# Block 2's scan: C multiplied by decays spread over the partitions, in place of products that are scaled and turned

## The reference

```python
a_cs = jnp.cumsum(aq, axis=2)
seg = a_cs[:, :, :, None] - a_cs[:, :, None]
decay = jnp.exp(jnp.where(lower, seg, -jnp.inf))
scores = jnp.einsum('bcqgn,bcsgn->bcqsg', Cq, Bq)
y_diag = jnp.einsum('bcqsg,bcqsgr,bcsgrp->bcqgrp', scores, decay, xq)
y_off = jnp.einsum('bcqgn,bcgrpn,bcqgr->bcqgrp', Cq, h_in, jnp.exp(a_cs))
...
y = y + xs.reshape(b, L, SSD_HEADS, SSD_HEAD_DIM) * d_skip[:, None]
y = rms_norm_2(y * jax.nn.silu(z), g_ssd)
return jnp.concatenate([fourier_mix(u_f), y], axis=-1) @ w_out
```

## Time and profile before

| | |
|---|---|
| Time, median of 3 runs | 1623.92 us (1622.88 to 1626.29) |
| Profiled execution: own time, span | 1624.92 us, 1622.4 us |
| PE busy, weight loads | 1607.2 us (99%), 1541.8 us |
| DVE, ACT, POOL busy | 1293.1, 923.2, 210.2 us |
| Granted clock of PE | 0.999 |
| The scan on PE | 1372.54 to 1393.25 us of the span |

### The profile page before, as it was taken

The page is one execution under the profiler, slowest core; times in us unless marked ns, Lnnn a source line. Parts: engine busy times, 40 slices in busy tenths (PEclk is TensorE's granted clock), DMA queues, the critical chain, the costliest instruction groups (busy, mean ns, idle before and its releaser), DMA issues.

```text
span 1622.4 us, 29880 instructions
## 1 busy us (share of the span) xinstructions
PE 1607.2 (99%) x13136; PEld 1541.8 (95%) x13136; DVE 1293.1 (80%) x1463; ACT 923.2 (57%) x1096; POOL 210.2 (13%) x122
## 2 busy tenths in 40 slices
PE   8999999999999999999999999999999999999998
PEld 8999988999999999999987899999999989899998
DVE  8887878687889888897878688885999597796655
ACT  7554655684465455545556686464655567554544
POOL 1000100000040001200000000032323368400000
PEclk9999999999999999999999999999999999999999
DMA  8667654444566765776754444555555434235552
GB/s 296 229 259 279 246 181 168 146 155 158 214 229 235 269 250 199 267 260 254 282 184 165 147 157 156 185 219 191 190 201 182 145 118 155 79 131 190 200 186 75
DMA packets 47520, 317.56 MB, mean 196 GB/s; under 512 B 5280, under 2 KB 8096, under 8 KB 9888
## 3 DMA queue, kind: packets, MB, share of 16 engines
q1 hardware_dynamic: 47248, 315.64, 53.3%
q10 hardware_dynamic: 144, 0.02, 0.0%
HBM read 314.60 MB, written 1.05 MB: 195 GB/s over the span
## 4 chain that ended last, share of the span: by engine, by line
PE 82%; DVE 9%; ACT 4%; POOL 2%; DMA 1%; issue 1%; SPq 0%; DVEq 0%; ACTq 0%
PE ps L1170 23%; PE ps L1172 23%; PE ps L1171 23%; PE ps L1368 3%; PE ps L1370 3%; PE ps L1369 3%; DVE wlo L1844 2%; ACT whi L648 1%; DVE pre L2455 1%; DMA raw<-in_w_dram 1%; PE ps L1382 1%; DVE dA_rows L1844 1%; DVE tmp L1844 1%; PE ps L1393 1%; DVE qkA L1844 1%
## 5 line engine op out<-in xcount | busy, mean ns | idle before, releaser
L1844 DVE TENSOR_TENSOR wlo<-raw,whi 128x2048 fp32r<-128x2048 f32 (+1 forms) x256 | 585.0, 2293 | 92.8 <-ACT whi L648 89.3
L648 ACT ACTIVATE whi<-raw 128x2048 fp32r<-128x2048 f32 (+1 forms) x264 | 499.9, 1905 | 216.9 <-DMA raw<-in_w_dram 216.9
L1170 PE MATMUL ps<-h1hi,whi 128*128 128x256 f32 x1792 | 500.8, 279 | 2.9 <-DVE wlo L1844 2.9
L1172 PE MATMUL ps<-h1lo,whi 128*128 128x256 f32 x1792 | 496.7, 277 | 0.0
L1171 PE MATMUL ps<-h1hi,wlo 128*128 128x256 f32 x1792 | 496.6, 277 | 0.0
L1170 PEld LDWEIGHTS ps<-h1hi,whi 128*128 128x128 f32 x1792 | 337.0, 188 | 7.1 <-issue 4.2
L1172 PEld LDWEIGHTS ps<-h1lo,whi 128*128 128x128 f32 x1792 | 337.1, 188 | 0.0
L1171 PEld LDWEIGHTS ps<-h1hi,wlo 128*128 128x128 f32 x1792 | 336.8, 188 | 0.1
L1170 PE MATMUL ps<-hid_hi,whi 128*128 128x256 f32 x880 | 244.0, 277 | 0.0
L1172 PE MATMUL ps<-hid_lo,whi 128*128 128x256 f32 x880 | 243.4, 277 | 0.0
L1171 PE MATMUL ps<-hid_hi,wlo 128*128 128x256 f32 x880 | 243.4, 277 | 0.0
(11 more groups left out here) (363 smaller groups left out, 2536.5 us busy)
## 6 DMA issues: line engine op xcount, KB each, us to landing
raw<-in_w_dram SPq DMA_DIRECT2D x288, 1024.0 KB, 4.8
raw<-in_w_dram SPq DMA_DIRECT2D x8, 256.0 KB, 5.4
c_rows<-in_c_rows_dram SPq DMA_DIRECT2D x2, 1024.0 KB, 9.9
relbias<-in_relbias_dram SPq DMA_DIRECT2D x2, 1024.0 KB, 8.5
pv<-in_pv_dram SPq DMA_DIRECT2D x2, 641.0 KB, 7.5
xT<-in_x_dram SPq DMA_DIRECT2D x4, 256.0 KB, 4.6
raw<-in_w_dram SPq DMA_DIRECT2D x2, 512.0 KB, 7.1
ctxT<-in_ctx_dram SPq DMA_DIRECT2D x1, 1024.0 KB, 6.9
```

The costliest lines, as they stand in the source:

```text
L648: act.activation(whi[:, slot, c], raw[:, slot, c], ACT.Copy).then_inc(hi_done[slot], 1)
L1170: pe.matmul(out, w_hi, hi, start=start, stop=False, skip_group_check=skip)
L1172: return pe.matmul(out, w_hi, lo, start=False, stop=stop, skip_group_check=skip)
L1844: return dve.tensor_tensor(out, a, b, op)
```

## The change

- The running decays are no longer taken as 48 columns (`tail_x[:, 48:96]`), but as rows: after chunk 11's segments PE makes 12 x 512 sums in bank 7, ACT takes their exponentials (`decay_rows`), SP writes them to a DRAM tensor and reads them back spread over all 128 partitions, in four transfers of 3, 3, 2 and 1 heads and a fifth of 3 heads behind a wait for the last segment sums (`seg_done` 6). A head's 4 x 128 decays are 256 KB over the partitions, so three heads are 768 KB.
- The decays take one place of the weight ring: a pseudo slab (`FILL`) stands in the stream behind b2+10 and its slot is given back by carried(3). Slab b2+11 and all later ones move one slot on, and b2+11 is loaded behind the five transfers.
- DVE multiplies C by the decays (`c_decay(g)`, heads 3g to 3g+2, both operands in SBUF, in place): g = 0 after conv(11), g = 1 after conv(12) and `z_clamp(0)`, g = 2 behind `cut_lo(b2 + 11)`, g = 3 behind `h1_ready`.
- `carried(e)` becomes 12 products by head that accumulate in y's banks. `carried_scale`, `turned` and `yoff` are gone. PE's order is cb, carried(0) to carried(3), within(0), within(1), then within(2) and within(3) in turns of four heads.
- The skip term's product moves from DVE to ACT (six ACTIVATEs on `xs_t`); DVE's add becomes one instruction for two tiles.
- Orders: ACT's `cut_hi` of b2+11, W0, W1, W2 comes one odd chunk later each and W3's behind `z_sigmoid(2)`; POOL does z's first gate ahead of `xdt`; DVE does `z_clamp(1)` ahead of W0's `cut_lo`, all four `within_weights` (with `z_clamp(2)` behind the third) ahead of W1's.

```diff
+DECAYS = (None, 0)
-    after = {}
+    after = {BLOCK2_0 + 10: DECAYS}
@@ SP
+                if i == FILL:
+                    sp.wait_ge(decay_rows_ready, 1)
+                    sp.dma_start(decay_dram, decay_rows[0:NH, :, :].rearrange("h e n -> h (e n)")).then_inc(decays_moved, 16)
                 if n > 0:
                     sp.wait_ge(used[slot], n)
+                if i == FILL:
+                    sp.wait_ge(decays_moved, 16)
+                    spread(0, 3, landed[slot])
+                    spread(3, 6, block2_landed)
+                    spread(9, 11, block2_landed)
+                    spread(11, 12, block2_landed)
+                    sp.wait_ge(seg_done, 6)
+                    spread(6, 9, decays_moved)
@@ POOL
+        z_gate(0)
         for tt in range(ST):
             ...
-        for j in range(3):
-            ...
+        z_gate(1)
+        cut_lo(b2 + WOUT20 + 2)
+        z_gate(2)
         cut_lo(b2 + WOUT20 + 3)
@@ ACT
+                if c == 11:
+                    act.wait_ge(sums_done, 2)
+                    act.activation(decay_rows[0:NH, :, :].rearrange("h e n -> h (e n)"), ps[0:NH, 7, :], ACT.Exp)\
+                       .then_inc(decay_rows_ready, 1)
             if c == 19:
                 conv_sigmoid(NCONV - 1)
                 z_sigmoid(0)
-        cut_hi(b2 + WOUT20 + 3)
+            if c % 2 == 1 and c > 1 and c != 15:
+                cut_hi(b2 + c // 2 + (4 if c < 15 else 3))
+        cut_hi(b2 + WOUT20 + 2)
         z_sigmoid(1)
-        z_sigmoid(2)
+        for m in range(XC):
+            ins = act.activation(xs_t[:, m, :], xs_t[:, m, :], ACT.Identity, scale=vec2("d_skip")[:, m:m + 1])
+        ins.then_inc(base_ready, 1)
         slab_used(act, b2 + WOUT20 - 1)
         act.activation(hhi[:, 0:2, :], u_t[:, :, :], ACT.Copy).then_inc(ycat_hi_ready, 1)
+        z_sigmoid(2)
+        cut_hi(b2 + WOUT20 + 3)
@@ PE
+            if c == 11:
+                pe.wait_ge(tail_ready, 2)
+                sums = ((dAx[0][:, f_], LE), (dAx[0][:, b_], GE), (dAx[1][:, f_], LE), (dAx[1][:, b_], GE))
+                for e, (lhs, rhs) in enumerate(sums):
+                    ins = pe.matmul(ps[0:NH, 7, e * P:(e + 1) * P], lhs, rhs, start=True, stop=True)
         def carried(e):
             tt, d = e // 2, e % 2
+            for h in range(NH):
+                if e == 0 and h % 3 == 0:
+                    pe.wait_ge(c_decayed, h // 3 + 1)
+                ins = pe.matmul(y_out(h, tt), hstate[:, d, (tt if d == 0 else 1 - tt), 64 * h:64 * h + 64],
+                                c_from_start(h, e), start=(e == 0 and h % 4 < 2), stop=False, skip_group_check=True)
+            if e == 3:
+                ins.then_inc(used[fill], 1)
         pe.wait_ge(uz_evac, 8)
+        for e in range(4):
+            carried(e)
         pe.wait_ge(xdt_ready, 1)
+        within(0, range(NH))
+        within(1, range(NH))
+        for first in range(0, NH, 4):
+            within(2, range(first, first + 4))
+            within(3, range(first, first + 4)).then_inc(y_done, 1)
@@ DVE
+        def c_decay(g):
+            dve.wait_ge(conv_silu, 11 + g)
+            ...
+            for first, n in ((3 * g, 3),) if g < 3 else ((9, 2), (11, 1)):
+                v = from_start[first]
+                for tt in range(ST):
+                    part = v[:, :, 2 * tt:2 * tt + 2, :]
+                    c = c_t[:, g, tt * P:(tt + 1) * P].unsqueeze(1).unsqueeze(1).to_broadcast([P, n, 2, P])
+                    ins = tt_(part, part, c, ALU.mult)
+            ins.then_inc(c_decayed, 1)
         for e in range(4):
-            if e == 3:
-                ycat_low(0, 0, u_t[:, :, :])
-            carried_scale(e)
             within_weights(e)
-            ...
+            if e == 2:
                 z_clamp(2)
+        cut_lo(b2 + WOUT20 + 1)
+        ycat_low(0, 0, u_t[:, :, :])
+        dve.wait_ge(base_ready, NCONV + 1)
         for j in range(XC // 2):
             dve.wait_ge(y_done, j + 1)
+            skip = xs_t[:, 2 * j:2 * j + 2, :].rearrange("p a b -> p (a b)")
+            done(tt_(skip, skip, ps[:, j, :], ALU.add))
```

More of the change, by code:

```diff
@@ L116 @@
 STREAM = weight_stream()
-PLACE = {g: i for i, (is_ada, g) in enumerate(STREAM) if not is_ada}
-ADA_PLACE = {a: i for i, (is_ada, a) in enumerate(STREAM) if is_ada}
+FILL = STREAM.index(DECAYS)
+PLACE = {g: i for i, (is_ada, g) in enumerate(STREAM) if is_ada is False}
+ADA_PLACE = {a: i for i, (is_ada, a) in enumerate(STREAM) if is_ada is True}
 SPLITS = {g: sum(1 for h in PLACE if PLACE[h] <= PLACE[g] and PLACE[h] % NS == PLACE[g] % NS) for g in PLACE}
@@ L325, in build_program @@
     xdt = at("xdt", [P, ST, 2, 768], F32, v0)
+    decay_rows = at("decay_rows", [P, 4, P], F32, h2)
+    slot0 = ring0 + FILL % NS * 4 * SLAB
+    from_start = {first: at(f"from_start{first}", [P, n, 4, P], F32, home)
+                  for first, n, home in ((0, 3, slot0), (3, 3, slot0 + 4 * NS * SLAB), (6, 3, dft0), (9, 2, h2), (11, 1, slot0 + 6144))}
+    decay_dram = nc.dram_tensor("decay_dram", [NH, 512], F32, kind="Internal").ap()
     dA_rows = [[at(f"dA_rows{tt}{d}", [P, NH, P], F32, first) for d, first in enumerate(homes)]
@@ L445, in build_program, with c_from_start @@
     Y_AT = {"b": 0, "a": 4, "c": 8}
+    fill = FILL % NS
+    def c_from_start(h, e):
+        first = max(k for k in from_start if k <= h)
+        return from_start[first][:, h - first, e, :]
     def slab_used(eng, g):
@@ L486, in _, with spread @@
         loaded = [3]
+        def spread(first, last, signal):
+            src = decay_dram[first:last, :].rearrange("h n -> (h n)").partition_broadcast(P)
+            sp.dma_start(from_start[first][:, :, :, :].rearrange("p h e n -> p (h e n)"), src).then_inc(signal, 16)
         def load(g):
@@ L1040, in _ @@
                 act.wait_ge(sums_done, 1)
[L1041 removed]
+                act.activation(tail_x, ps[:, 7, 128:176], ACT.Exp).then_inc(tail_ready, 1)
             if kind == "dt":
@@ L1717, in _, with y_out, within @@
         pe.wait_ge(h1_ready, 1)
+        def y_out(h, tt):
+            first = (h // 2 % 2) * S + tt * P
+            return ps[64 * (h % 2):64 * (h % 2) + 64, h // 4, first:first + P]
         def carried(e):
             tt, d = e // 2, e % 2
[L1722 to L1736, removed]
+            for h in range(NH):
[5 more added lines that the diff above has]
+                ins.then_inc(used[fill], 1)
+        def within(e, heads):
             tt, d = e // 2, e % 2
             pe.wait_ge(seg_ready, e + 1)
-            for h in range(NH):
-                out = ps[64 * (h % 2):64 * (h % 2) + 64, h // 4, (h // 2 % 2) * S + tt * P:(h // 2 % 2) * S + (tt + 1) * P]
-                ins = pe.matmul(out, xdt[:, tt, d, 64 * h:64 * h + 64], seg[e][:, h, :], start=False, stop=(d == 1),
+            for h in heads:
+                ins = pe.matmul(y_out(h, tt), xdt[:, tt, d, 64 * h:64 * h + 64], seg[e][:, h, :], start=False, stop=(d == 1),
                                 skip_group_check=True)
-                if e == 3 and h % 4 == 3:
-                    ins.then_inc(y_done, 1)
-        carried(0)
+            return ins
         for tt in range(ST):
@@ L2490, in _ @@
                 ins.then_inc(wx_ready, 1)
+            if j == 11:
+                c_decay(0)
             if j == 12:
                 z_clamp(0)
+                c_decay(1)
         cut_lo(b2 + 11)
+        c_decay(2)
         dve.wait_ge(states_done, 2)
@@ L2501, in _ @@
         ins.then_inc(h1_ready, 1)
+        c_decay(3)
+        z_clamp(1)
         cut_lo(b2 + WOUT20)
@@ L2716, in lay_out @@
            for i in ADA_COLS]
-    out["w"] = np.stack([ada[i] if is_ada else slabs[i] for is_ada, i in STREAM])
+    out["w"] = np.stack([ada[i] if is_ada else slabs[i] for is_ada, i in STREAM if is_ada is not None])
     out["gains"] = np.concatenate([cols_on_partitions(a[name][l]) for l in range(DEPTH)
```

58 lines of the change are left out of this document (19 added, 39 removed).

## The result

The changed kernel takes 1629.64 us (median of 7 runs, 1629.0 to 1630.81) against 1624.11 for the kernel before (median of 7 runs, 1622.88 to 1626.29): a ratio of 1.0036, interval 1.0027 to 1.0045, 5.5 us slower. The forecast was 1633.1, slower. In the profiled execution the span grows from 1622.4 to 1627.6.

What follows compares the result with a forecast made beforehand. PE was taken to bound the kernel, and in block 2's scan DVE's last gate to set the end. Gate 1406.35 against 1397.1, +9.2 us, took the median from 1623.92 to 1633.1; range 1619.0 to 1638.0, the forecast's own 1628 to 1637.

Steps and rivals of the forecast that it cites:

- The quantity: When DVE ends block 2's last gate, 1397.1 before; everything behind it was to move one for one.
- PE's gain: Block 2's scan on PE: 13.4 us of products against 20.7, 7.3 less if nothing is awaited.
- The lock and the turns: DVE instructions with two SBUF inputs and POOL's exclude each other for whole instructions, taking turns; c_decay pays for it.
- Walk, step by step: DVE's queue followed from c_decay(0) through POOL's turns to the last gate at 1406.35, +9.2 us.
- Stalls on PE: PE waits at chunk 22 (2.6), for h1 (2.5), in carried(0) (3.3) and for the fourth weights.
- Transfers: Decay spreads from DRAM: 4.8 us for the first, 3 more for each follower, at no cost to the time.
- The clock: PE's granted clock could fall behind its waits as well; it read 0.999 over the whole span before.
- the late decays: Rival: at 9.9 us a transfer the decays reach c_decay(1) 12.5 late; about 1645, chance 0.07.
- The signs: Forecast wrong if c_decay products last 0.9 to 1.0, PE's scan is under 20 us, or last gate precedes 1397.
- The fast rival: Lock costs little on DVE: last gate 1391.2, 5.9 us faster, 1618.0; chance 0.23.
- The walk without the lock: DVE's queue with all blocked times behind 1356.5 removed: h1 ends 1372.9, last gate 1391.2.

Runs made afterwards that it cites:

- psum_operand: Changed kernel with the c_decay products' second operand a PSUM constant and a maximum in place of the product, leaving C out: 1623.99 us, ratio 0.9998.
- pe_fill: Changed kernel with 9 unused products of ones on PE ahead of each of two waits (h1, last quarter of C): 1629.07 us, ratio 1.0029.
- before_reordered_2: Kernel before with W1's and u's low parts and z_clamp(2) later, W3 and ACT's rounding of u earlier, skip term's product on ACT: ratio 0.9994.
- before_w1_late: Kernel before with slab W1's low part made by DVE behind the last gate: 1622.4 us, ratio 0.9991.
- after_w1_late: Changed kernel with slab W1's low part made by DVE behind the last gate, PE's products with W1 behind those with W3: 1626.99 us, ratio 1.0022.

## Why the prediction was right, and where its size was off

- **The quantity.** The last gate's end was named as what everything follows. It moved by 5.4 us in the trace and the time by 5.5, with 5.6 behind it in both kernels. Right.
- **PE's gain.** 13.4 us of products were forecast; psum_operand shows 13.7 (cb 1.9, carried 5.5, within 6.3). Right to 0.3, and worthless by itself.
- **The lock and the turns.** Read from rows of the kernel before; shown by psum_operand, where a second operand in PSUM brought the gate from 37.9 to 32.8 with number, widths and order of the products kept. (They are ten, as the prediction's own sum has them, and not the eight that its text speaks of.) The trace of the changed kernel shows the turns at each place of the walk but one.
- **Walk, step by step** (forecast, measured): conv(12) starts 1360.65, 1359.78; conv(13)'s clamp ends 1370.55, 1368.75; h1 1378.1, 1376.07; c_decay(3) 1384.35, 1381.48; fourth weights 1395.0, 1391.77; last gate 1406.35, 1402.55. The overestimate of 3.8 us arises first in c_decay(0) and (1): the first began 0.6 earlier than taken (silu(10) was done at 1353.6, not 1354.2). In c_decay(1) no silu came between, since POOL stood 1.37 us waiting for ACT's sigmoid: 1.81 in place of 2.4. c_decay(3) took 5.49 in place of 6.25, the gates 10.8 behind the fourth weights in place of 11.35. Mis-sized were these turns, about 0.5 us at each of several meetings, all in one direction. 1629.64 still lies in the forecast's own range, 1628 to 1637.
- **Stalls on PE.** Forecast 2.6, 2.5, 3.3 and 2.5; measured 0.78, 2.12, 2.06 and 0.99. The places are right, each size too large by the same walk; the last was shortened by the clock, which kept carried busy for longer, as pe_fill shows (2.12 without).
- **Transfers.** Forecast at no cost. The DMA view of the changed kernel, 1325 to 1400, lists them (KB each, us from issue to landing):

```profile
from_start<-decay_dram SPq DMA_DIRECT2D x3, 768.0 KB, 5.3
from_start<-decay_dram SPq DMA_DIRECT2D x1, 512.0 KB, 6.9
from_start<-decay_dram SPq DMA_DIRECT2D x1, 256.0 KB, 7.1
```

  The first was issued at 1337.79 and no row of DVE waits for one. Slab b2+11 went out behind the fifth at 1350.61 (forecast 1350.7). Of the two ends, 4.8 was the right one.
- **The clock.** Named only beside the late decays, without a price. It fell; it cost nothing on the path.
- **The signs.** Of the three that were to show the forecast wrong, one came: the scan on PE is 18.0 us long (1376.21 to 1394.22), under 20. It was ill chosen, since the prediction's own walk has 19.4 (1378.1 to 1397.5): the waits stand ahead of cb as well as in the scan. The other two did not come, and conv(12), PE's waits and the gates showed what was named.
- **The fast rival** failed on its own point: far more than 5.9 of the 15.2 us were blocked, 11.35 by the last gate (1402.55 against that walk's 1391.2). Its number, 1618.0, would not have come out even without the lock: psum_operand reached 1623.99. The walk without the lock (gate at 1391.2) took it away everywhere, and W0's low part, `z_clamp(1)` and the gates stand behind POOL in that run too (3.56, 1.72 and 2.17 us, for 2.28, 0.43 and 0.69 alone).

Left open: no version that multiplies C outside the lock and computes the reference was tried, nor one that has the decays land in PSUM. What the added work, the transfers and the order cost apart from each other is open too. Whether the order of before_reordered_2 is really faster would need more executions than these.

## What to carry to other kernels

Before moving work onto DVE, look at where its operands live and at what POOL has queued at that time: some 7 us of products with two SBUF inputs beside POOL made the kernel 5 us slower than before, and with a PSUM operand it was back at its old time. Follow the queues of all engines to the point that everything behind depends on, and count a saving on PE only if DVE reaches that point sooner. When one wait is taken out, look for who is late next: in several of these runs microseconds that were won came back one or two instructions later.

## What was not expected of the hardware

- When POOL had instructions queued and DVE had products with two SBUF inputs, they alternated one by one in nearly every case with full products. Two products of 8 columns passed in one turn: the first took 2.34 us beside POOL's half slab, the second 0.15, and POOL's next half its usual 2.41. In both cases DVE's price of a meeting is what is left of POOL's instruction, and not the length of its own.
- `z_clamp` has one SBUF input and no second one, and was held as well: 0.43 us alone, 1.18 to 2.49 beside POOL's half slabs (changed kernel 1.18, psum_operand 1.56, before_w1_late 2.49). Products with one of two inputs in PSUM were not: `within_weights` took 1.74 beside them.
- In the changed kernel two waits of 2.1 us on PE, 3.3 us of products apart, were followed by two windows of 2 us at 0.62 and 0.52 of the clock; with 18 records of ones in each wait it stayed at 1.00. In after_w1_late the clock was at 0.50 behind the first such wait already.
- A spread of 768 KB from 6 KB in DRAM to 128 partitions landed 5.3 us after its issue (median of three), a slab of 1024 KB 4.8; the two smaller ones in between, of 512 and 256 KB, took 6.9 and 7.1.
